# Layer 1's adaptive sums as row products on VectorE during the first FFN, and four sum-filter taps of the convolution on TensorE

## The reference, cut

```python
silu_c, silu_cc = jax.nn.silu(c), jax.nn.silu(c_ctx)
for i in range(DEPTH):
    mod_x = (silu_c @ ada_w[i] + ada_b[i])[:, None, :]     # 6*1024 numbers: "adaptive sums"
    mod_c = (silu_cc @ ada_w[i] + ada_b[i])[None, None, :]
    sx1, cx1, gx1, sx2, cx2, gx2 = jnp.split(mod_x, 6, axis=-1)
    ...
def conv_module(h, ...):
    a, g = jnp.split(h @ pw1_w + pw1_b, 2, axis=-1)
    u = dwconv(a * jax.nn.sigmoid(g), dw_w, dw_b)           # 31 taps per channel
    return jax.nn.silu(layernorm(u, ln_g, ln_b)) @ pw2_w + pw2_b
```

## Time and profile before

| what | value |
| --- | --- |
| time, median of 3 runs | 1667.96 us (1667.38 to 1669.21) |
| the profiled execution | 1666.32 us |
| its span in the trace | 1664.5 us |
| TensorE busy | 1645.6 us, 99% |
| VectorE busy | 956.1 us, 57% |
| ScalarE busy | 675.9 us, 41% |
| GpSimd busy | 174.3 us, 10% |
| granted TensorE clock, mean | 0.998 |

### The profile page before, as it was taken

How to read it: one execution, slowest core, us unless ns; L and a number is a source line. 1 busy time by engine, 2 the same in 40 slices (tenths; PEclk the granted TensorE clock), 3 DMA queues, 4 the chain that set the end, 5 groups by cost and what they waited for, 6 DMA issues and landing times.

```text
span 1664.5 us, 25807 instructions
## 1 busy us (share of the span) xinstructions
PE 1645.6 (99%) x10126; PEld 1437.0 (86%) x10126; DVE 956.1 (57%) x1498; ACT 675.9 (41%) x1015; POOL 174.3 (10%) x190
## 2 busy tenths in 40 slices
PE   8999989999999999999999999999999999999998
PEld 6777758998888888888899999999999888888888
DVE  6999987753433332234358665756566754543445
ACT  4656667632323222223354433324145533332334
POOL 1488841000000000000000000000000000000001
PEclk9999999999999999999999999999999999999999
DMA  9666642121222112212113120212112223232321
GB/s 384 233 236 246 252 190 79 62 86 38 73 70 72 54 63 65 67 59 69 45 52 94 63 76 33 83 51 70 57 59 78 97 88 117 89 100 89 101 88 52
DMA packets 40729, 165.74 MB, mean 100 GB/s; under 512 B 5089, under 2 KB 6369, under 8 KB 34497
## 3 DMA queue, kind: packets, MB, share of 16 engines
q1 hardware_dynamic: 38384, 151.55, 26.5%
q0 software_dynamic: 2256, 12.98, 2.2%
HBM read 162.41 MB, written 2.10 MB: 99 GB/s over the span
## 4 chain that ended last, share of the span: by engine, by line
PE 78%; DVE 5%; ACT 2%; issue 0%; DVEq 0%; ACTq 0%
PE ps L663 78%; DVE rstd L1637 1%; DVE H_lo L1672 1%; DVE w_lo L1631 1%; DVE tmp L1660 1%; DVE sq L1660 0%; DVE rstd L1648 0%; ACT sq L1230 0%; DVE X L1995 0%; ACT tmp L1230 0%; ACT H_hi L1221 0%; DVE H_lo L1670 0%; ACT tmp L1358 0%; DVE conv L2108 0%; PE ps L1076 0%
## 5 line engine op out<-in xcount | busy, mean ns | idle before, releaser
L663 PE MATMUL ps<-H_hi,w_hi 128*128 128x512 f32 (+1 forms) x1712 | 582.9, 340 | 4.0 <-DVE H_lo L1670 2.7
L663 PE MATMUL ps<-H_lo,w_hi 128*128 128x512 f32 (+1 forms) x1712 | 578.4, 338 | 0.0
L663 PE MATMUL ps<-H_hi,w_lo 128*128 128x512 f32 (+1 forms) x1712 | 577.9, 338 | 0.0
L663 PEld LDWEIGHTS ps<-H_hi,w_hi 128*128 128x128 f32 x1712 | 324.6, 190 | 57.2 <-issue 19.1
L663 PEld LDWEIGHTS ps<-H_hi,w_lo 128*128 128x128 f32 x1712 | 324.5, 190 | 35.1
L663 PEld LDWEIGHTS ps<-H_lo,w_hi 128*128 128x128 f32 x1712 | 324.8, 190 | 34.4
L1631 DVE TENSOR_TENSOR w_lo<-w_raw,w_hi 128x1024 fp32r<-128x1024 f32 x208 | 255.2, 1239 | 107.8 <-ACT w_hi L1183 74.8
L663 PE MATMUL ps<-mid_hi,w_hi 128*128 128x512 f32 (+1 forms) x592 | 199.4, 337 | 0.5
L663 PE MATMUL ps<-mid_lo,w_hi 128*128 128x512 f32 (+1 forms) x592 | 198.1, 335 | 0.0
L663 PE MATMUL ps<-mid_hi,w_lo 128*128 128x512 f32 (+1 forms) x592 | 198.1, 335 | 0.0
L2139 DVE SCALAR_TENSOR_TENSOR tmp<-ps,par,tmp 128x511 f32<-128x511 f32 x66 | 41.6, 657 | 231.3 <-ACT tmp L1516 155.0
(11 more groups left out here) (277 smaller groups left out, 2109.6 us busy)
## 6 DMA issues: line engine op xcount, KB each, us to landing
w_raw<-in_w_units SPq DMA_DIRECT2D x190, 512.0 KB, 3.5
ada<-in_ada_groups SPq DMA_DIRECT2D x38, 1024.0 KB, 6.4
w_raw<-in_w_units SPq DMA_DIRECT2D x16, 384.0 KB, 3.3
ada<-in_ada_groups POOLq DMA_DIRECT2D x4, 1024.0 KB, 10.5
ada_more<-in_ada_groups POOLq DMA_DIRECT2D x4, 1024.0 KB, 13.3
X<-in_x_cols SPq DMA_DIRECT2D x4, 768.0 KB, 7.5
w_raw<-in_w_units POOLq DMA_DIRECT2D x2, 512.0 KB, 14.2
ada_half<-in_ada_groups POOLq DMA_DIRECT2D x1, 1024.0 KB, 19.3
```

The source lines that it names most:

```text
L663: return nc.tensor.matmul(o, a, b, start=first, stop=last, skip_group_check=True)
```

## The change

Four things are changed.

1. Layer 1's adaptive sums leave the group scheme. Of 24 groups 12 are left (layer 0), and a block of the convolution's loop takes one, behind its value unit. `ada_w[1]` is laid out transposed, in 48 tiles of 128 x 1024 (`ada_cols`), and in the first FFN VectorE multiplies a tile with a row of `silu(c)` or `silu(c_ctx)` and sums along the row: `MOD_JOBS` lists 64 such jobs (tiles 0 to 15 for both vectors, 16 to 47 for `c` alone). They run behind `mid_lo` of blocks 1 to 21: three a slot, four in the last. Each job's tile is loaded by a DMA from GpSimd's queue into one of two buffers; the load waits for the job two before. Tiles 0 to 15 are loaded twice.
2. Layer 1's `modulation` runs behind the last job, and both VectorE and ScalarE wait for it ahead of the third chunk's out phase.
3. In blocks 0 to 6 the sum filter's first four taps are TensorE matmuls against diagonals (`first_sums`), which ACT makes (`sum_diagonals`); ACT then adds the bias in PSUM, and VectorE goes on from tap 4. The order of taps and weight splits on VectorE and of splits, copies and products on ScalarE changes accordingly.
4. VectorE's pairs of the first FFN are written out instead of looped, and the last iteration of TensorE's loop too; a few small tiles move in memory.

```diff
+PE_SUM = 4
+MOD_TILES = 48
+MOD_BUFS = 2
+MOD_JOBS = [(j, v) for j in range(2 * KT) for v in range(2)] + [(j, 0) for j in range(2 * KT, MOD_TILES)]
+MOD_SLOTS = FT - 1
@@ sync @@
-                for m in (2 * b + 5, 2 * b + 6):
-                    if m < 24:
-                        load_group(m)
+                if b + 5 < 12:
+                    load_group(b + 5)
@@ gpsimd @@
+            pool.wait_ge(h_lo_ready, KT * PARTS_BEFORE[3])
+            for v in range(2):
+                pool.dma_start(silu_rows[v], c_rows[v:v + 1, :].to_broadcast([P, D])).then_inc(c_rows_in, 16)
+            for n, (j, _) in enumerate(MOD_JOBS):
+                if n >= MOD_BUFS:
+                    pool.wait_ge(mod_job, n - MOD_BUFS + 1)
+                pool.dma_start(mod_tile[:, n % MOD_BUFS, :], ada_cols[j]).then_inc(mod_tile_in[n % MOD_BUFS], 16)
@@ tensor @@
+            def first_sums(b):
+
+                pe.wait_ge(sum_diag_ready, PE_SUM * (b + 1))
+                pe.wait_ge(both_ready, b + 1)
+                for n in range(PE_SUM):
+                    m = mm(sum_acc, sum_diag[:, n, :], both_phases[:, n:n + HALF], n == 0, n == PE_SUM - 1)
+                m.then_inc(sum_seeded, 1)
+            first_sums(0)
...
-                        if h == 0:
-                            ada_transposes(4 * i + (2 * q + 3))
-                            ada_products(4 * i + (2 * q + 4))
-                    ada_transposes(4 * i + (2 * q + 4))
-                    ada_products(4 * i + (2 * q + 5))
+                    ada_transposes(2 * i + (q + 3))
+                    ada_products(2 * i + (q + 4))
+                    if not (isinstance(i, int) and b == KT - 1):
+                        first_sums(b)
...
-                    ada_transposes(19)
-                if j == KT - 1:
-                    ada_products(20)
+                    ada_transposes(11)
...
-            ada_transposes(20)
...
-            ada_products(21)
...
-                    if n in (3, 5, 9):
-                        ada_transposes(21 + t)
-                    if n in (3, 5):
-                        ada_products(22 + t)
@@ scalar @@
+            def sum_diagonals(b):
+
+                for n in range(PE_SUM):
+                    A(sum_diag[:, n, :], ident[:], ACT.Copy, scale=sum_weight(n, b)).then_inc(sum_diag_ready, 1)
...
+                split_hi(2 * b + 4, (2 * b + 4) % RING)
                 act.wait_ge(slot_read[0], S_PW1 // 2 + b + 1)
...
-                products(b, range(0, 6))
-                ada_copy(2 * b + 5)
-                split_hi(2 * b + 4, (2 * b + 4) % RING)
-                products(b, range(6, 11))
+                products(b, range(0, 4))
+                if b < KT - 1:
+                    act.wait_ge(sum_seeded, b + 1)
+                    A(sum_acc, sum_acc, ACT.Identity, bias=sum_w[:, ODD_TAPS * KT + b:ODD_TAPS * KT + b + 1]) \
+                        .then_inc(sum_biased, 1)
+                if b:
+                    ada_copy(b + 4)
+                products(b, range(4, 11))
...
-                if b + 1 < KT:
-                    ada_copy(2 * b + 6)
+                if b + 1 < KT - 1:
+                    sum_diagonals(b + 1)
...
+                        act.wait_ge(mod_ready, 14)
                         out_phase_norm(blk, s, x_at, both, layer, 40, 3 + 2 * layer)
@@ vector @@
-                taps(b, range(0, LEAD))
-                ada_sum(4 + 2 * b, 0, 4 + b)
-                taps(b, range(LEAD, 6))
                 split_lo(2 * b + 4, (2 * b + 4) % RING)
-                taps(b, range(6, 12))
-                ada_sum(5 + 2 * b, 1, b)
-                taps(b, range(12, 14))
-                split_lo(2 * b + 5, (2 * b + 5) % RING)
-                taps(b, range(14, EVEN_TAPS))
+                even_tap(b, 0)
+                if b:
+                    ada_sum(b + 3, 0, b + 3)
+                even_tap(b, 1)
+                for j in range(PE_SUM, EVEN_TAPS):
+                    sum_tap(b, j)
+                    if j - PE_SUM + 2 < DVE_EVEN:
+                        even_tap(b, j - PE_SUM + 2)
+                    if j == EVEN_TAPS - 5:
+                        split_lo(2 * b + 5, (2 * b + 5) % RING)
...
+            def mod_jobs(slot):
+
+                for n in range(len(MOD_JOBS) * (slot - 1) // MOD_SLOTS, len(MOD_JOBS) * slot // MOD_SLOTS):
+                    j, c = MOD_JOBS[n]
+                    buf = mod_tile[:, n % MOD_BUFS, :]
+                    dve.wait_ge(silu_rows_ready, 2)
+                    dve.wait_ge(mod_tile_in[n % MOD_BUFS], 16 * (n // MOD_BUFS + 1))
+                    v.tensor_tensor_reduce(buf, buf, silu_rows[c], 1.0, 0.0, ALU.mult, ALU.add,
+                                           accum_out=mod[:, 1, j, c:c + 1]).then_inc(mod_job, 1)
...
+                            if both and f + 2 * i + q:
+                                mod_jobs(f + 2 * i + q)
...
+                        modulation(len(MOD_JOBS), 1, 0, 48, 11)
+                        dve.wait_ge(mod_ready, 14)
                         out_phase_norm(blk, s, x_at, both, 3 + 2 * layer)
```

More of the change, by code:

```diff
@@ L361, in backbone @@
         last_row = sem("last_row")
+        sum_diag_ready = sem("sum_diag_ready")
+        sum_seeded = sem("sum_seeded")
+        sum_biased = sem("sum_biased")
+        c_rows_in = sem("c_rows_in")
+        silu_rows_ready = sem("silu_rows_ready")
+        mod_tile_in = [sem(f"mod_tile_in{n}") for n in range(MOD_BUFS)]
+        mod_job = sem("mod_job")
         stat_sq_pool = sem("stat_sq_pool")
@@ L1523, in pairs @@
                             A(mid_hi[:, ds(2 * i + q, 1), 0:w], m32[:, q:q + 1, 0:w], ACT.Copy).then_inc(mid_hi_ready, 1)
+                            if both and c_no == 0 and isinstance(i, int) and q == 0:
+                                act.wait_ge(c_rows_in, 16 * 2)
+                                for v in range(2):
+                                    A(silu_rows[v], silu_rows[v], ACT.Silu).then_inc(silu_rows_ready, 1)
                     if c_no == 0:
@@ L1693, in modulation @@
             def modulation(m, layer, t0, t1, at):
-                dve.wait_ge(mod_sum, m + 1)
+                if layer == 0:
+                    dve.wait_ge(mod_sum, m + 1)
+                else:
+                    dve.wait_ge(mod_job, m)
                 v.tensor_tensor(mod[:, layer, t0:t1, :], mod[:, layer, t0:t1, :],
@@ L1835, in even_tap @@
                         dve.wait_ge(conv_ready, b - 1)
-                    v.scalar_tensor_tensor(tap_even[:, b % 2, :], frm, w, even_acc, ALU.mult, ALU.add)                         .then_inc(even_ready, 1)
+                    v.scalar_tensor_tensor(tap_even[:, b % 2, :], frm, w, even_acc, ALU.mult, ALU.add) \
+                        .then_inc(even_ready, 1)
                     dve.wait_ge(even_ready, b + 1)
-            def taps(b, js):
-                for j in js:
-                    sum_tap(b, j)
-                    if j >= LEAD:
-                        even_tap(b, j - LEAD)
             def last_block(b):
-                made = (DVE_STEPS - 2) * b
+                made = steps_made[0]
                 at = {}
@@ L1954, in _ @@
             last_rows(KT - 1)
-            modulation(18, 0, 16, 48, 8)
+            modulation(11, 0, 16, 48, 8)
             v.tensor_tensor(pw2_gb[:], mod[:, 0, 16:24, :], two(par[:, PW2_B:PW2_B + KT]), ALU.mult) \
@@ L2128, in pairs @@
                         for q in range(2):
-                            if not (isinstance(i, int) and q == 0):
+                            if not (c_no == 0 and isinstance(i, int) and i + q == 0):
                                 split_lo(4 * i + (2 * blk + 2 * q + 3), (2 * q + 3) % RING)
@@ L2154, in pairs @@
                                 .then_inc(mid_lo_ready, 1)
-                    if c_no == 0:
-                        pairs(0)
-                    with dve.Fori(1 if c_no == 0 else 0, n // 2) as i:
-                        pairs(i)
+                            if both and f + 2 * i + q:
+                                mod_jobs(f + 2 * i + q)
+                    if both:
+                        for i in range(n // 2):
+                            pairs(i)
+                    else:
+                        if c_no == 0:
+                            pairs(0)
+                        with dve.Fori(1 if c_no == 0 else 0, n // 2) as i:
+                            pairs(i)
                     f += n
@@ L2366, in laid_out @@
     first = w[0][:, 0:2 * D].reshape(D, 2, FIRST_GROUPS, 2 * P).transpose(0, 2, 1, 3).reshape(D, 2 * D)
-    both = np.concatenate([first, w[0][:, 2 * D:], w[1]], axis=1)
-    groups = np.ascontiguousarray(both.reshape(2, KT // 2, P, 24, GROUP * P).transpose(3, 0, 2, 1, 4)
-                                  .reshape(24, 2, P, KT // 2 * GROUP * P))
-    return [("x_cols", x_cols), ("params", params), ("ada_groups", groups)]
+    whole = np.concatenate([first, w[0][:, 2 * D:]], axis=1)
+    groups = np.ascontiguousarray(whole.reshape(2, KT // 2, P, 12, GROUP * P).transpose(3, 0, 2, 1, 4)
```

(4 more changed lines are left out.)

95 lines of the change are left out of this document (42 added, 53 removed).

## The result

The changed kernel took 1686.49 us (median of 4 runs, 1685.84 to 1690.17), beside 1667.67 for the kernel before on the same chip: a ratio of 1.012, 95% interval 1.0105 to 1.0134. The forecast was 1666.5, its range ended at 1671.0. The change makes the kernel 1.2% slower.

A forecast was written before the change was run, and what follows sets the result against it. VectorE was taken to bound the convolution's loop by half a microsecond a block, TensorE after the change. -2.2 - 0.6 + 0 + 1.3 = -1.5 us gave 1666.5 against the median of 1667.96; range 1662.0 to 1671.0.

The forecast's parts named there:

- The loop: Convolution's loop: VectorE's block falls from 22.2 to 19.9 us, TensorE bounds at 21.91; -2.2 us, bounds 0 and -3.4.
- Is there a wait within this?: Convolution's loop: `first_sums` doesn't wait for the phases if VectorE finishes its block by V; 0.9 us left over.
- Rival 3: Convolution's loop: phases, sums, bias and taps wait for each other, a microsecond a block, 1672 us; chance 10%.
- Layer norm, second projection: Behind the loop: groups 20 to 23 go, two reductions and four transposes leave the chain; -0.6 us, bounds -0.3 and -5.
- Rival 4: Layer norm: TensorE's queue limits there too, removed groups count in full, -5 instead of -0.6 us, 1662; chance 12%.
- Jobs: First FFN: a slot's jobs and load take 6.5 us within 8.07 of VectorE's idle time; 0 us, bounds 0 and 8.7 a slot.
- Rival 2: First FFN: a job costs about 2.3 us by the half-rate rule, the end +4.3 instead of +1.3, 1669.5 us; chance 12%.
- Rival 1: First FFN: loads above 5.5 us make the jobs overrun the slot, about 1705 us at a load of 8; chance 8%.
- The end of the FFN: First FFN's last slot: four jobs, then modulation, delay ScalarE's read, TensorE goes on at 829.2; +1.3 us, bounds 0 and +4.
- Rival 5: End of the first FFN: costs nothing, loads take 3 us and ScalarE's wait is hidden, 1665 us; chance 10%.

The follow-up runs named there:

- experiment 1: Changed kernel with ScalarE making the high half of unit 2b+5 among its products, ahead of the next gate's sigmoid: 1671.92 us, ratio 1.0031.
- Experiment 4: experiment 1 with three tile buffers for the jobs instead of two and the four-job slot first instead of last: 1668.62 us, ratio 1.0005.
- experiment 5: Experiment 4 with the 64 tile loads issued by ScalarE instead of GpSimd, ScalarE's first-FFN pairs written out: 1666.86 us, ratio 0.9992.
- experiment 3: Two kernels: changed kernel without the 64 jobs and loads, 1684.46 us (1.0101); experiment 1 with two sum taps on TensorE instead of four, 1674.65 us (1.0044).

## Why the prediction was wrong

**The loop: the step that failed.** It is the paragraph that asks "Is there a wait within this?". It counted VectorE's block from the value unit's end V: phases at V + 1.3, tap 4 at V + 5.8, "12 pairs of 1.07 and a weight split of 1.14 follow", ready at V + 20.0 with "0.9 us left over". The work was right: 19.55 us against 19.9. The sentence failed in its condition, "as long as VectorE has finished its block by V": in the block shown V is 126.58 and VectorE begins its read at 128.83, 2.25 us late, and in all six blocks of the loop it is 2.2 to 3.0 us late. The reason is a wait inside the block that was put at nothing. The weight split has an input, the high half, and it was put in as a duration without asking when that is there. ScalarE makes it behind the next block's gates, that is behind the gate unit, and the change makes the gate unit start only after the phases (`first_sums` stands ahead of it). The wait of 0.46 us for a high half in the FFN was a hint at how near ScalarE's halves come. The ring, from one start of the phase sum to the next, by VectorE's, TensorE's and ScalarE's timelines over 130.44 to 154.42: the sum of the phases until TensorE starts on it 0.73, four taps and the gate unit 11.24 (131.17 to 142.41), sigmoid 0.94, three products 1.54, four diagonals 1.18, high half 1.08, low half 1.14, four tap pairs with the last two taps 4.52, the two reads 1.61: 23.98 us, and measured are 24.0. Seven of these nine terms stand in the prediction or in its rows of before; they were never added round the circle.

**Rival 3** ("the loop's ring closes: phases, sums, bias and taps wait for each other") named this, with too small a chance, 10%, and too small a price. It took a microsecond a block as lateness by itself, 6 us. By the starts of the phase sums, six blocks lost 2.2 us each against the 21.8 of experiment 1. Three of them lost more: the first another 0.8, since `first_sums` waits there for the first diagonals; the second another 1.65, where the clock fell (25.65 us from 81.53 to 107.18, at a mean granted clock of 0.93); the fifth another 0.8, with a weight split of 1.97 us instead of 1.23. The last block lost 1.05, and 1.05 came back ahead of the first and behind the last of these marks. Together 16.4, which makes +14.15 of -2.25. Its mechanism was also told too loosely (bias, GpSimd) to be checked; the one link that mattered was not in it.

**Layer norm, second projection (-0.6)**: -0.45 in the changed kernel and -0.6 in experiment 1 (225.25 to 313.78 there, 227.50 to 316.62 before). Right in sum. The part put down to two reductions did not show at `H_lo` (+14.15 at the sums, 281.14 to 295.24 = +14.10); all of it came with the transposes. Rival 4 is out: two groups never counted in full.

**Jobs: 0.** Right. 1.15 a job instead of 1.3; the load from release to use took 403.46 - 399.15 = 4.3 instead of 3.9; 1.63 us of idle time left where 1.5 was said. Rival 2, a job of 2.3 us, is out: a job over 1024 elements takes 1.22 us, exactly the weight split's time. The Trainium skill's page "Vector Engine (DVE) Microarchitecture Reference" (section "Points that are easy to get wrong") has two non-bf16 SBUF sources halve the throughput of an `S2S2D2_STT`; the 1.22 us show no such halving, though no run shows whether the job is an instruction of that form. The fit of the Trainium skill's page "DMA: Bandwidth & Descriptors" (section "Anatomy of one DMA — SWDGE (gpsimd) path") gave an estimate of 3.2 us for a load; the page of the profile has a median of 3.8. Rival 1 is out.

**The end of the FFN: +1.3** was +1.8. The mechanism is the one named; the term that was too small is the load of the fourth tile:
```profile
834.35 1.22 DVE L2145 CUSTOM_DVE_ANT_0 mod_tile<-mod_tile,sq 128x1024 f32<-128x1024 f32 x1
838.64 1.23 DVE L2145 CUSTOM_DVE_ANT_0 mod_tile<-mod_tile,sq 128x1024 f32<-128x1024 f32 x1 [3.06 <-DMA mod_tile<-in_ada_cols]
840.48 1.23 DVE L2145 CUSTOM_DVE_ANT_0 mod_tile<-mod_tile,sq 128x1024 f32<-128x1024 f32 x1 [0.60 <-DMA mod_tile<-in_ada_cols]
```
Released by the second job (834.35 + 1.15 = 835.50) it is used at 840.48, 4.98 us later, where 3.9 was put; the third tile took 4.29. Two loads beside each other took longer than the one of the sum. The jobs were 0.35 shorter than said in this chain and the last `mid_lo` came 0.25 sooner in its slot. Experiment 4 shows a further cost that the sum had no term for: in experiment 1 the clock fell behind this wait, for 1.65 us more. In the changed kernel it did not fall there. Rival 5, an end that costs nothing, is out.

**What no step held.** 2.3 us behind the last store, shown by experiment 5. The +0.96, +0.54 and +0.53 of the table, 2.0 together, have the size that the kernel before showed when its buffers were shifted (3.0), but only for the first is it shown that addresses make it: from the first FFN's start to the third chunk's last slot the kernels take 494.6 us (before), 495.6 (changed), 495.75 (experiment 4), and 493.9 with 32 bytes more. The 0.54 behind the third chunk stays in every kernel with the change at whatever offset, and the kernel before shows 0.9 there with either unused row. The last stretch, where the 0.53 lies, took 25.41 and 24.88 us in two executions of one and the same kernel, so a single pair of traces can't tell it. Together with the loop (16.35 off), the end (0.5) and the layer norm (0.15) this gives 21.3, and -1.5 + 21.3 = 19.8.

## What to carry to other kernels

Where a change puts a wait into an in-order queue, write down for every instruction behind it not only how long it takes but when its inputs are ready, engine by engine and round the loop until the chain meets itself; a block in which no engine is full afterwards is a ring, and moving one call may be the whole cure. Tiles that are loaded for a later job need a buffer for each job of a slot, or the slot pays a load's full latency inside it. And when small buffers are cut or moved, note at which offset the large ones start before and after: a comparison of two kernels can carry 3 us that belong to neither idea.

## What the runs showed of the hardware that was not expected

- **Where the buffers start in SBUF changes TensorE's pace.** 32 unused bytes a partition made the kernel before slower by 3.0 us (1.0018) and 64 made it faster by 2.1 (0.9988, interval 0.9979 to 0.9998); a unit over `mid_hi` and `mid_lo` took 6.24 to 6.36 us at the same granted clock.
- **Loads issued by GpSimd cost 2.3 us at the program's end**, long after the last of them: 5.45 us from the last store's issue to the end of the span with 64 of them, 3.2 without them or with ScalarE issuing them. The kernel before, with over twenty loads by GpSimd, has 3.2; where between the two counts it begins, or whether their place in the kernel matters, was not tried.
- **A short wait on TensorE can cost nearly its length again in clock.** Behind idle time of 2.07 us the granted clock read 0.72 of full over 6 us, a mean of its two levels (1.2 and 2.4 GHz), and 1.65 us more were lost; behind the wait of 1.82 us in the changed kernel, and of 1.90 in experiment 3's with two taps, it stayed at full. In the changed kernel's loop TensorE waited five times for 2.14 or 2.15 us, and the clock fell behind the first of these alone, and not behind a sixth wait of 2.90 us. So the length of the wait doesn't decide it; what does is open.
- **The multiply-and-sum over 1024 float32 elements from two SBUF rows** takes 1.22 us on VectorE, with 0.08 for the accumulator's read; one follows the other after 1.15.
